# A two-layer streaming-encoder trunk: the low weight part made by GpSimd in two operations of 512 columns instead of one of 1024

## What is computed

```python
for layer in range(DEPTH):                      # DEPTH = 2
    if layer % 2 == 0:
        x = x + rglru_sgu_mixer(rms_norm(x, norm_ab[e]), w_in_ab[e], ...)
    else:
        x = x + chunk_band_attention(rms_norm(x, norm_attn[o]), w_qkv[o], rel_bias[o], w_o[o])
    x = x + conv_ffn(rms_norm(x, norm_ffn[layer]), ffn_w_up[layer], ffn_conv_w[layer],
                     ffn_conv_b[layer], ffn_w_down[layer])
return rms_norm(x, norm_final)
```

## Time and profile before

| what | us |
|---|---|
| median of 3 runs | 1182.83 (1182.06 to 1182.88) |
| span of the profiled execution | 1180.5 |
| TensorE busy | 1130.1 (96%) |
| VectorE busy | 729.0 (62%) |
| GpSimd busy | 474.2 (40%) |
| ScalarE busy | 440.7 (37%) |

### The profile page before, as it was taken

One profiled execution on the slowest core, in us unless ns is written; L12 is line 12 of the kernel. 1 busy time (PEld: TensorE's weight loads), 2 busy tenths in 40 slices (PEclk: granted clock), 3 DMA queues, 4 the chain that ended last, 5 costly groups with the idle time before them and its releaser, 6 DMA issues.

```text
span 1180.5 us, 15574 instructions
## 1 busy us (share of the span) xinstructions
PE 1130.1 (96%) x5215; PEld 920.4 (78%) x5215; DVE 729.0 (62%) x1155; ACT 440.7 (37%) x674; POOL 474.2 (40%) x210
## 2 busy tenths in 40 slices
PE   7998799999999999999999999989999999999996
PEld 5886578888888887788777777768888888887886
DVE  5879866766666752223777777675766767651123
ACT  5283343332322332223455555544323223232221
POOL 4343443444444444443332222143544444444442
PEclk8998899999999999999999999999999999999998
DMA  7372222332322332332323222122323232233302
GB/s 267 104 227 72 71 89 72 109 106 89 103 92 95 100 104 96 103 107 89 107 72 103 77 71 75 51 72 72 125 89 107 89 99 97 91 105 107 100 25 72
DMA packets 37587, 115.08 MB, mean 97 GB/s; under 512 B 4752, under 2 KB 7440, under 8 KB 37552
## 3 DMA queue, kind: packets, MB, share of 16 engines
q1 hardware_dynamic: 35376, 110.41, 28.0%
q10 hardware_dynamic: 2176, 4.19, 1.1%
HBM read 112.19 MB, written 6.59 MB: 101 GB/s over the span
## 4 chain that ended last, share of the span: by engine, by line
PE 75%; DVE 7%; issue 5%; ACT 3%; DVEq 0%; ACTq 0%
PE bank L1120 24%; PE bank L1121 23%; PE bank L1122 23%; PE bank L1413 1%; PE bank L1430 1%; DVE p_sb L1029 1%; PE bank L1428 1%; DVE acc L728 1%; ACT p_sb L614 1%; PE bank L1311 1%; DVE o_sb L1046 1%; ACT o_sb L639 0%; DVE x L1112 0%; ACT oh L647 0%; DVE small L1026 0%
## 5 line engine op out<-in xcount | busy, mean ns | idle before, releaser
L358 POOL TENSOR_TENSOR wl<-raw,wh 128x1024 fp32r<-128x1024 f32 x191 | 463.8, 2430 | 679.0 <-ACT wh L413 679.0
L1120 PE MATMUL bank<-xh,wh 128*128 128x512 f32 x1008 | 401.4, 398 | 7.4 <-DVE xl L721 6.6
L1121 PE MATMUL bank<-xl,wh 128*128 128x512 f32 x1008 | 394.0, 391 | 0.0
L1122 PE MATMUL bank<-xh,wl 128*128 128x512 f32 x1008 | 394.0, 391 | 0.0
L413 ACT ACTIVATE wh<-raw 128x1024 fp32r<-128x1024 f32 x191 | 202.0, 1059 | 384.9 <-PE bank L1122 339.1
L1120 PEld LDWEIGHTS bank<-xh,wh 128*128 128x128 f32 x1008 | 190.3, 189 | 51.5 <-DVE xl L721 7.3
L1122 PEld LDWEIGHTS bank<-xh,wl 128*128 128x128 f32 x1008 | 190.2, 189 | 40.6
L1121 PEld LDWEIGHTS bank<-xl,wh 128*128 128x128 f32 x1008 | 190.5, 189 | 36.9
L1120 PE MATMUL bank<-ah,wh 128*128 128x512 f32 (+1 forms) x357 | 136.2, 381 | 0.0
L1121 PE MATMUL bank<-al,wh 128*128 128x512 f32 (+1 forms) x357 | 134.4, 376 | 0.0
L1122 PE MATMUL bank<-ah,wl 128*128 128x512 f32 (+1 forms) x357 | 134.4, 376 | 0.0
(11 more groups left out here) (193 smaller groups left out, 1131.7 us busy)
## 6 DMA issues: line engine op xcount, KB each, us to landing
raw<-weights SPq DMA_DIRECT2D x191, 512.0 KB, 3.3
bias_scratch<-ext_scratch SPq DMA_DIRECT2D x1, 4096.0 KB, 19.0
bias<-bias_scratch ACTq DMA_DIRECT2D x8, 512.0 KB, 3.6
x<-x_in SPq DMA_DIRECT2D x8, 256.0 KB, 5.4
out<-x SPq DMA_DIRECT2D x4, 384.0 KB, 3.0
raw<-weights SPq DMA_DIRECT2D x2, 256.0 KB, 3.4
out<-x SPq DMA_DIRECT2D x2, 256.0 KB, 2.2
lng<-ln_g SPq DMA_DIRECT2D x1, 256.0 KB, 9.9
```

What stands on the lines that cost most here:

```text
L358: nc.gpsimd.tensor_tensor(wl[:, c % RING].rearrange("p k c -> p (k c)"), raw[:, c % RAW], wh[:, c % RING].rearrange("p k c -> p (k c)"), A ...
L1120: nc.tensor.matmul(dst, w_hi_part, m_hi, start=first, stop=False)
L1121: nc.tensor.matmul(dst, w_hi_part, m_lo, start=False, stop=False)
L1122: return nc.tensor.matmul(dst, w_lo_part, m_hi, start=False, stop=last)
```

## The change

split_lo makes each unit's low part in two GpSimd operations of 512 columns (FIRST = 512) where it was one of 1024. Only the second one signals w_lo. Nothing waits between the two, and no other engine's program is changed. Unit 0 was already made in two halves (lines 370 and 373) and stays so. The rest of the diff is blank lines.

```diff
             def split_lo(c, turn=0):
                 pool.wait_ge(w_hi, c + 1 + RAW * turn)
-                nc.gpsimd.tensor_tensor(
-                    wl[:, c % RING].rearrange("p k c -> p (k c)"), raw[:, c % RAW],
-                    wh[:, c % RING].rearrange("p k c -> p (k c)"), ALU.subtract).then_inc(w_lo, 1)
+                low, high = (w[:, c % RING].rearrange("p k c -> p (k c)") for w in (wl, wh))
+                nc.gpsimd.tensor_tensor(low[:, 0:FIRST], raw[:, c % RAW, 0:FIRST], high[:, 0:FIRST], ALU.subtract)
+                nc.gpsimd.tensor_tensor(low[:, FIRST:], raw[:, c % RAW, FIRST:], high[:, FIRST:],
+                                        ALU.subtract).then_inc(w_lo, 1)
```

## The result

The changed kernel takes 1171.76 us (median of 4 runs, 1169.82 to 1172.31); the kernel before, four runs, 1182.86 us (1182.06 to 1183.16). The ratio is 0.9909 with a 95% interval of 0.9897 to 0.9921: 11.1 us faster, against the 13.9 forecast. The span of the profiled execution went from 1180.5 to 1170.4 us, and the mean granted clock is 0.985 in both. (One number ahead of the prediction is off by one: there are 192 weight units, unit 0 and the 191 of the loop, not 193.)

What follows compares the result with a forecast made beforehand. TensorE, fully busy in feed-forward, was elsewhere held up by VectorE, which GpSimd excludes for whole operations. Terms -2.8 - 1.1 - 2.2 - 1.7 - 5.4 - 0.7 = -13.9 us took 1182.8 to 1168.9 us, range 1165.5 to 1178.

Steps and rivals of the forecast that it cites:

- The decisive step: VectorE gets its turn between GpSimd's two halves, so the most a VectorE operation can wait is halved.
- (c): GpSimd keeps its turn over both halves, VectorE waits as before, no gain: 1182.8 us; chance 0.08.
- (d): No turn between halves and each holds its own 1.29 us, so slower: 1190 us; chance 0.07.
- Term 1: Mixer: VectorE operations held by GpSimd units end earlier, -2.8 us, bounds 0 and 3.2.
- Term 2: Fourth output tile: the addition TensorE waits for comes earlier, its 1.13 us idle time is won, -1.1 us.
- Term 3: QKV head: low parts of q and k end earlier, TensorE's 2.78 us idle shrink to some 0.5, -2.2 us.
- Term 4: Behind the QKV head's idle time: no 3.3 us at clock 0.50, -1.7 us; other bound 0.
- Term 5: Eight pairs of heads: last 256-column scaling held less, mainly in five pairs, -5.4 us, bounds 1.2 and 6.6.
- rival (a): Pairs of heads: GpSimd comes ahead of the last but one scaling, each half holds one: 1173.1 us; chance 0.18.
- Term 6: Attention's output projection: awaited unit 0.6 us late, additions behind it earlier, -0.7 us, bounds +0.6 and -1.0.
- rival (b): Longer pause at 779.24 (2.9 us) lets the clock fall, costing 1.7 to 2.6 us more: 1171.1 us; chance 0.10.
- Both rivals together: rival (a) in the pairs and rival (b) at the output projection both come true: 1175.3 us, inside the range.

Runs made afterwards that it cites:

- whole units and the later copy: Kernel before, with ScalarE in each pair of heads copying q first and making the weight unit's high part (weight copy) behind it: 1175.81 us, ratio 0.9942.
- halves and the later copy: Changed kernel, with ScalarE in each pair of heads copying q first and making the weight unit's high part (weight copy) behind it: 1166.23 us, ratio 0.9860.
- the delay of 256 columns: Changed kernel with an added ScalarE copy of 256 columns, needed by no result, ahead of the weight copy in each pair of heads: 1166.06 us, ratio 0.9863.

## Why the prediction was right, and where it wasn't

**The decisive step held.** That VectorE gets its turn between two halves rested on three operations of the final norm. The rows of the QKV head above show it for the weight units, and rivals (c) and (d) fall with it; the kernel with halves from unit 96 on shows that each place keeps its gain. Where no VectorE operation that GpSimd can hold up is between, two halves follow each other at 302.86 and 304.11 and the unit is done in 1.25 + 1.28 = 2.53 us instead of 2.40; the estimate from unit 0 had been 0.12 to 0.18 more, and it is 0.13.

**Term 1, mixer: 2.8 forecast, 3.35 measured,** 3.6 counted from the start, which in this execution lies 0.25 us later because the second half of unit 0's load landed later. The first restart is 1.26 us ahead where I had 1.0. The low part of y takes 1.57 us instead of 2.65, as the rule of the single victim says. The 3.35 us hang on which two executions were profiled. In the other traces whose mixer has the same instructions, the restart lies at 141.93 and 142.32 with whole units and at 136.83, 137.23, 137.24 and 137.77 with halves: the means are 4.5 us apart, and 3.35 is the least that any two of them give.

**Term 2: 1.1 forecast, the 1.13 us are gone.** **Term 3: 2.2 forecast,** and the pause went from 2.78 to 0.61 us: 2.17. **Term 4: 1.7 forecast,** and from 552 to 560 us the clock is at 1.00; the lead from the QKV head to the first waiting pair grows by 2.60, of which that pair's own pause gives 1.09, so the clock gave some 1.5. But that the fall belongs to the pause was never sure. The kernel with whole units and the later copy has the same pause and no fall (its restart, and its busy time around it, the clock before the last two columns):

```profile
563.19 0.50 PE L1397 MATMUL bank<-kh,qh 64*128 64x512 f32 x2 [2.79 <-DVE kl L1000]
```

```profile
562.00:570.00 8.00, 6.81 (x44) 5.01 (x45) 6.19 (x24) 3.84 (x12) 3.38 (x2) 1.00 0.62 219
```

So term 4 came true in this pair of executions; taking all of it, with 0 as a mere bound, was in part luck.

**Not forecast: about 1.1 us of clock behind the mixer.** The pause there is 5.0 us in both kernels, and TensorE restarts at 0.50. Before, the clock stayed low until 147.4, 5.7 us behind the restart; now until 141.8, 3.5 us behind it. The busy time of the 6 us behind each restart shows it, of before and of the changed kernel (the clock stands before the last two columns):

```profile
142.00:148.00 6.00, 6.00 (x16) 4.66 (x16) 0.91 (x2) 0.63 (x1) 0.00 (x0) 0.55 0.27 87
```

```profile
138.00:144.00 6.00, 5.68 (x18) 4.59 (x19) 2.64 (x3) 0.63 (x1) 1.40 (x1) 0.68 0.27 87
```

Half of the 2.2 us less at half speed is 1.1 us of work. 3.35 + 1.13 + 1.1 + 2.17 = 7.75, against the 7.95 us measured at the QKV head. The halves aren't the reason: the kernel with halves and the later copy, with the changed kernel's mixer, needs 6.0 us behind the same pause (137.24 to 143.3), and the one with whole units and the later copy, with the mixer of before, only 3.2 us (142.32 to 145.5). So this 1.1 us is luck of the two executions that were profiled.

**Term 5, pairs of heads: 5.4 forecast, 1.09 + 0.46 = 1.55 measured.** This is the term that failed, by 3.85 us. It is rival (a), to which I gave 0.18. Its failed step is the sentence that ScalarE and VectorE hang on the same scores, so that their distance should stay. The margin was 0.07 us, and the distance moved by 0.14. The timeline of ScalarE suggests the cause. Before, the last accumulator read ahead of the second pair's weight copy ended at 626.03 and the copy began at 626.14, a gap of 0.11 us:

```profile
625.84 0.19 ACT L614 ACTIVATION_READ_ACCUMULATOR p_sb<-p_sb,small 128x1 f32 x1
626.14 1.06 ACT L413 ACTIVATE wh<-raw 128x1024 fp32r<-128x1024 f32 x1
```

In the changed kernel the copy follows directly (615.50, 615.46):

```profile
615.31 0.19 ACT L576 ACTIVATION_READ_ACCUMULATOR p_sb<-p_sb,small 128x1 f32 x1
615.46 1.06 ACT L377 ACTIVATE wh<-raw 128x1024 fp32r<-128x1024 f32 x1
```

Counted from the restart of the pair ahead (605.97 and 595.42) the copy starts at 20.17 before and 20.04 after, and GpSimd at 21.31 and 21.18, while the last but one scaling, which VectorE's own chain sets, starts at 21.24 and 21.25. Besides ScalarE's own work the copy hangs on the load and on TensorE, which releases the slot, so I read the gap as a short wait for TensorE. In the last pair of the trace of before the gap is longer and the profile names who ended it:

```profile
732.76 1.06 ACT L413 ACTIVATE wh<-raw 128x1024 fp32r<-128x1024 f32 x1 [0.19 <-PE bank L1122]
```

The halves had made one TensorE step of the pair 0.09 to 0.13 us earlier (its scores at 617.43 and 606.75 lie 11.46 and 11.33 us behind the restart), because the low part for it was held for less long; VectorE's chain didn't follow, since one of its later operations, the low part of the attention's output (line 1054 before), has both halves ahead of it, and two halves in a row hold 0.14 us longer than a whole. So the change itself moved the coincidence on which its gain in the pairs stood. That this order decides is shown by the delay of 256 columns, which brings the term back; why the copy came 0.13 us sooner is read from these rows and wasn't tried. The gap of 0.11 us and the row of 732.76 stood in the trace of before, and I hadn't asked what ended it.

**Term 6, output projection: 0.7 gain forecast, 0.5 us lost.** The pause is 2.86 us where I had said 2.9, and the additions behind it do come earlier; the mechanism was right. But rival (b), 0.10, came true as well: behind 2.86 us the clock fell for 3.4 us, 1.7 us of work. With unit 120 whole both are gone, though the clock need not be the unit's doing, as the experiment on that unit says. In the final norm the clock is low from 1159.0 on, 11.4 us before the end, where it was 9.1 us before; that takes another 0.3 us.

**Both rivals together had been put at 1175.3,** and it became 1171.8. Of the 3.5 us between, the mixer and the clock behind it gave 0.55 + 1.1 more than their terms, term 5 kept 1.55 where rival (a) left 1.2, term 6 lost 0.5 where rival (b) would have had it lose 1.0 to 1.9, term 4 gave 0.2 less and the final norm 0.3 less, the profiled execution's own 1172.31 lies 1.9 us above its span instead of 2.3, and the median lies 0.5 us below it. That adds up to 3.0 to 3.9 us. So the range held, but by another case than the likeliest: both rivals (0.18 and 0.10, with no chance given to the pair) came true, and some luck of the clock took part of their cost back. The single figure forecast was 2.9 us too low.

**Feed-forward stages at nothing:** right, as the 400.90 of 401.00 us show.

## What to carry to other kernels

Where two engines exclude each other for whole instructions, cut the instructions of the one that isn't on the path, down to where its own total begins to be waited for (here four and eight parts can't be told apart). The one unit that the bounding engine waits for itself may be worth keeping whole: with halves that won, with quarters it is within the noise. A term that rests on who comes first by less than some tenths of a microsecond isn't a term: ask for both neighbours what releases them, since the change will move one of them, and count the other order as equally likely. A few hundred ns of delay at the right place, even of useless work, can then be worth more than the change.

## What the runs showed of the hardware

- GpSimd gives way at the end of each of its instructions, without any wait between them, and a further instruction has a small price: an undisturbed unit of 1024 columns takes 2.40 us in one operation, 2.53 in two, 2.83 in four, 3.39 in eight, about 0.14 us for each further one.
- With GpSimd making 8 of 1024 columns, VectorE's same 1155 instructions took 616.7 us instead of 729.0, and the kernel 47 us less; part of the 47 can come from units that are ready sooner.
- In the pairs of heads a scaling of 256 columns takes 0.35 us with GpSimd 0.06 us or more behind its start, and 1.3 to 1.5 us with GpSimd's half 0.04 us behind it or ahead.
- The clock fell to 0.50 behind a pause of 2.78 us in the kernel before and of 2.86 in the changed one, and not behind one of 2.79 with whole operations and the later copy. It did not fall behind one of 2.27 in the kernel before and in both with unit 120 whole, and did behind one of 2.27 at 770.28 with whole operations and the later copy (0.53 from 770 to 772 us, 1.00 from 774). So a pause's length alone doesn't decide it. Behind pauses of 5.02 to 5.04 us at the end of the mixer it came back after 3.2 and 5.7 us with whole operations, after 3.5 and 6.0 with halves.
- The chain of waits of the changed kernel gives GpSimd 22% of the span, while TensorE is busy 400.90 of 401.00 us in feed-forward 0, where nothing could be won from a faster GpSimd. So a share in the chain isn't a gain.
